# A sixth expert buffer, used once, in the room of the token rows and the last gate

## What is computed

```python
# gates: sigmoid routing, top 8 of 64 experts for each token, plus one shared expert
act = silu(einsum('nd,edf->nef', t, w_gate_e)) * einsum('nd,edf->nef', t, w_up_e) * gates[:, :, None]
routed = einsum('nef,efd->nd', act, w_down_e)
x = x + m[:, 5] * (routed + shared)        # m[:, 5] is "the last gate"
y = rmsnorm(x, final_g)
```

## Time and profile before

| what | us |
|---|---|
| median of three runs | 889.63 |
| lowest and highest of them | 885.89 and 891.04 |
| the profiled execution | 885.69 |
| its span, first to last instruction | 883.9 |
| PE busy | 836.7 (95%) |
| DVE busy | 478.7 (54%) |
| ACT busy | 234.9 (27%) |

### The profile page before, as it was taken

One profiled execution on the slowest core, in us unless ns is written; L12 is line 12 of the kernel. 1 busy time (PEld: TensorE's weight loads), 2 busy tenths in 40 slices (PEclk: granted clock), 3 DMA queues, 4 the chain that ended last, 5 costly groups with the idle time before them and its releaser, 6 DMA issues.

```text
span 883.9 us, 13285 instructions
## 1 busy us (share of the span) xinstructions
PE 836.7 (95%) x4926; PEld 492.6 (56%) x4926; DVE 478.7 (54%) x994; ACT 234.9 (27%) x384; POOL 87.7 (10%) x201
## 2 busy tenths in 40 slices
PE   4799999999999999999999999999999999999993
PEld 2387886889999874444444444444444443444441
DVE  1563373586667456145746454554645454555575
ACT  2537643444423241211111111111111111112122
POOL 7420000000001161000000000000000000000000
PEclk9899999999999999999999999999999999999997
DMA  9984877822244378489999999999999999999951
GB/s 360 353 281 159 315 262 281 195 95 96 96 143 165 158 292 322 178 358 420 421 417 422 418 420 419 419 419 421 419 419 420 419 421 417 421 419 419 420 238 71
DMA packets 70988, 283.06 MB, mean 320 GB/s; under 512 B 14340, under 2 KB 30784, under 8 KB 43920
## 3 DMA queue, kind: packets, MB, share of 16 engines
q1 hardware_dynamic: 55344, 260.06, 73.6%
q0 software_dynamic: 6880, 17.64, 5.4%
q10 hardware_dynamic: 8704, 4.54, 2.0%
HBM read 281.40 MB, written 5.53 MB: 325 GB/s over the span
## 4 chain that ended last, share of the span: by engine, by line
PE 77%; DMA 16%; DVE 3%; issue 1%; POOL 1%; ACT 1%; SPq 0%; POOLq 0%; DVEq 0%; ACTq 0%
PE bank L1444 22%; DMA gu<-in_w_up_e_dram 11%; PE bank L1463 10%; PE bank L1472 8%; PE bank L1074 8%; PE bank L1076 7%; PE bank L1075 7%; DMA chunk_raw<-in_w_ada_dram 3%; PE bank L1432 3%; PE bank L1096 2%; PE bank L1129 1%; DMA h_dram<-h_row 1%; PE bank L1360 1%; PE bank L1552 1%; DMA xg<-h_dram,slot_tok 1%
## 5 line engine op out<-in xcount | busy, mean ns | idle before, releaser
L1444 PE MATMUL bank<-gu,x_t 128*32 128x512 f32 (+2 forms) x1440 | 233.6, 594 | 7.1 <-DMA gu<-in_w_up_e_dram 6.7
L1444 PEld LDWEIGHTS bank<-gu,x_t 128*32 128x32 f32 (+2 forms) x1440 | 74.5, 122 | 149.0 <-issue 143.4
L2068 DVE TENSOR_TENSOR ffn_acc<-ffn_acc,bank 128x512 f32<-128x512 f32 x186 | 116.5, 682 | 7.8 <-PE bank L1472 6.8
L1463 PE MATMUL bank<-dn,a_t 128*32 128x512 f32 (+2 forms) x720 | 120.3, 596 | 0.0
L1036 ACT ACTIVATE silu_sb<-bank 128x256 f32<-128x256 f32 x33 | 12.7, 385 | 320.3 <-PE bank L1444 320.3
L2010 DVE TENSOR_TENSOR act_sb<-silu_sb,bank 128x256 f32<-128x256 f32 x33 | 13.9, 421 | 148.2 <-ACT silu_sb L1036 148.2
L1074 PE MATMUL bank<-h_hi,chunk_lo 128*128 128x384 f32 x240 | 84.0, 350 | 0.0
L1076 PE MATMUL bank<-h_hi,chunk_hi 128*128 128x384 f32 x240 | 80.6, 336 | 0.0
L1075 PE MATMUL bank<-h_lo,chunk_hi 128*128 128x384 f32 x240 | 80.4, 335 | 0.0
L447 DVE TENSOR_TENSOR chunk_lo<-chunk_raw,chunk_hi 128x2048 fp32r<-128x2048 f32 x25 | 57.1, 2289 | 41.5 <-ACT chunk_hi L441 41.3
L2060 DVE SCALAR_TENSOR_TENSOR y_lo<-bank,slot_gate,y_hi 128x512 fp32r<-128x512 f32 x66 | 49.4, 748 | 54.4 <-ACT y_hi L1026 54.2
(11 more groups left out here) (349 smaller groups left out, 1018.2 us busy)
## 6 DMA issues: line engine op xcount, KB each, us to landing
gu<-in_w_gate_e_dram SPq DMA_DIRECT2D x64, 1024.0 KB, 18.6
gu<-in_w_up_e_dram SPq DMA_DIRECT2D x64, 1024.0 KB, 22.3
dn<-in_w_down_e_dram SPq DMA_DIRECT2D x64, 1024.0 KB, 21.6
chunk_raw<-in_w_ada_dram SPq DMA_DIRECT2D x24, 1024.0 KB, 9.0
chunk_raw<-in_w_in_dram SPq DMA_DIRECT2D x18, 1024.0 KB, 6.6
chunk_raw<-in_w_out_dram SPq DMA_DIRECT2D x4, 1024.0 KB, 5.2
chunk_raw<-in_w_pa_dram SPq DMA_DIRECT2D x2, 1024.0 KB, 5.1
chunk_raw<-in_w_pb_dram SPq DMA_DIRECT2D x2, 1024.0 KB, 5.2
```

What stands on the lines that cost most here:

```text
L1444: mm = pe.matmul(bank[2 + odd(u, first)][at_x, :].rearrange("p (g n) -> p g n", g=2), x_t[:, cols], wide[:, :, k, :], start=(k == 0), stop ...
L1463: mm = pe.matmul(outs[half][at_x, :], a_t[:, cols], dn[slot_of(x, first)][:, wc], start=(k == 0), stop=(k == 1))
L2068: dve.tensor_tensor(ffn_acc[t][:, cols], ffn_acc[t][:, cols], out[:, :], ALU.add).then_inc(S["place_out"], 1)
```

## The change

A sixth buffer, `gu_once` and `dn_once` (number RING = 5), is laid over `x_sb`, `gate_ffn` and `final_g_sb`: each of gate and up takes 8 KB and each half of down 4 KB, in two pieces 24 KB apart. It is used for expert x = 3 alone, the fourth that SP loads. All later experts of the first group take the ring's buffers one place earlier in turn, so that expert 5 gets the shared expert's buffer and expert 6 the one of expert 0. From expert 9 on each expert waits for the same predecessor as before.

For that the tokens' rows are stored to a new DRAM tensor `x_dram` (three DMAs on SP's queue behind the first nine loads), and `load_gu` of expert 3 waits for these stores and for `xhat2`. In the last group, behind all gate and up loads and all but the last two down loads, SP loads the last gate, the three token tiles and `final_g` into their places (3 MiB in all; gate and final_g in buffer 2, once expert 10 of that group is done with it). `sums_in` waits for all five. POOL's and ACT's early loads of the two are gone.

```diff
+        gu_once = at("gu_once", [P, 2, 6 * D], 0)
+        dn_once = at("dn_once", [P, 2, 6 * D], 8)
...
+        gate_ffn = at("gate_ffn", [P, 2, D], ring[2])
+        final_g_sb = at("final_g_sb", [P, D], ring[2] + 8)
...
-        SLOT0 = [(0, 3, 1, 4, 2)[x % RING] for x in range(EPG0)]
-        SLOT = [(0, 3, 1, 4, 2)[(EPG0 + x) % RING] for x in range(EPG)]
+        IN_TURN, ONCE = (0, 3, 1, 2, 4), 3
+        SLOT0 = [RING if x == ONCE else IN_TURN[(x - (x > ONCE)) % RING] for x in range(EPG0)]
+        SLOT = [IN_TURN[(EPG0 - 1 + x) % RING] for x in range(EPG)]
...
+                    elif k == RING:
+                        sp.wait_ge(S["xhat2"], TT)
+                        sp.wait_ge(S["out_stored"], 16 * TT)
...
+            for t in range(TT):
+                sp.wait_ge(S["out_done"], TT + t + 1)
+                sp.dma_start(x_dram[t * P:(t + 1) * P, :], x_sb[:, t, :]).then_inc(S["out_stored"], 16)
             sp.wait_ge(S["passes_ready"], 1)
...
+            free = max(x for x in range(EPG) if SLOT[x] == 2)
+            sp.wait_ge(S["gu_used"], last_group(passes) * EPG + (EXPERTS_AHEAD + free + 1))
+            sp.sem_inc(S["turn_step"], 1)
+            sp.dma_start(gate_ffn[:, :, :], gate_dram[:, D:2 * D].unsqueeze(0).to_broadcast([P, 2, D])).then_inc(S["ffn_gate_loaded"], 16)
+            for t in range(TT):
+                sp.dma_start(x_sb[:, t, :], x_dram[t * P:(t + 1) * P, :]).then_inc(S["ffn_gate_loaded"], 16)
+            sp.dma_start(final_g_sb[:, :], final_g.rearrange("(a n) -> a n", a=1).to_broadcast([P, D])).then_inc(S["ffn_gate_loaded"], 16)
             for x, n in sides_of(BPG - 1, False):
                 load_dn(x, last_group(passes), expert_at(bass.ds(last_group(passes) * (2 * BPG) + (SEQ_AHEAD + n), 1)))
...
-            pool.wait_ge(S["w_mm"], NPROJ)
-            spread_rows(gate_ffn, 1, S["ffn_gate_loaded"])
...
-            act.dma_start(final_g_sb[:, :], final_g.rearrange("(a n) -> a n", a=1).to_broadcast([P, D])).then_inc(S["late_loaded"], 16)
...
-                dve.wait_ge(S["ffn_gate_loaded"], 16)
+                dve.wait_ge(S["ffn_gate_loaded"], 16 * (TT + 2))
```

More of the change, by code:

```diff
@@ L265, in hybrid_step @@
         ffn = [at(f"ffn{t}", [P, D], EX + 4 * t) for t in range(TT)]
-        squared = [at(f"squared{t}", [P, D], EX + 24 + 4 * t) for t in range(TT)]
+        gate_ffn = at("gate_ffn", [P, 2, D], ring[2])
+        final_g_sb = at("final_g_sb", [P, D], ring[2] + 8)
+        squared = [at(f"squared{t}", [P, D], EX + 36 + 4 * t) for t in range(TT)]
         place_r = at("place_r", [P, NTOK], EX + 112, F32R)
@@ L329, in hybrid_step @@
         rows_loaded = [sem(f"rows_loaded{t}") for t in range(TT)]
-        gu_ready = [sem(f"gu_ready{i}") for i in range(RING)]
-        dn_ready = [sem(f"dn_ready{i}") for i in range(RING)]
+        gu_ready = [sem(f"gu_ready{i}") for i in range(RING + 1)]
+        dn_ready = [sem(f"dn_ready{i}") for i in range(RING + 1)]
         block = ctx.enter_context(nc.Block())
@@ L526, in load_dn @@
                     sp.wait_ge(S["dn_used"], group * EPG + (EXPERTS_AHEAD + y + 1))
-                    sp.sem_inc(S["sp_turn"], 1)
-                sp.dma_start(dn[k][:, :], w_down_e[0, e].rearrange("a (p k) n -> (a p) (k n)", k=2)).then_inc(dn_ready[k], 16)
+                    sp.sem_inc(S["turn_step"], 1)
+                src = w_down_e[0, e]
+                if k == RING:
+                    sp.dma_start(dn_once[:, :, 0:D], src.rearrange("a (p k) n -> (a p) k n", k=2)).then_inc(dn_ready[k], 16)
+                else:
+                    sp.dma_start(dn[k][:, :], src.rearrange("a (p k) n -> (a p) (k n)", k=2)).then_inc(dn_ready[k], 16)
             def expert_at(n):
@@ L1440, in gate_up @@
                     for x in experts:
-                        wide = gu[slot_of(x, first)][:, :].rearrange("p (g k n) -> p g k n", g=2, n=FE)
+                        wide = gate_up_part(slot_of(x, first))
                         for at_x in tiles_of(x, u, first):
@@ L1459, in down @@
                         for x in experts:
-                            wc = slice(k * D + 512 * half, k * D + 512 * half + 512)
                             for at_x in tiles_of(x, u, first):
                                 cols = slice(k * CAP + at_x.start, k * CAP + at_x.stop)
-                                mm = pe.matmul(outs[half][at_x, :], a_t[:, cols], dn[slot_of(x, first)][:, wc], start=(k == 0), stop=(k == 1))
+                                mm = pe.matmul(outs[half][at_x, :], a_t[:, cols], down_part(slot_of(x, first))[:, k, 512 * half:512 * half + 512], start=(k == 0), stop=(k == 1))
                             if half == 1 and k == 1:
```

27 lines of the change are left out of this document (15 added, 12 removed).

## The result

| | before | after |
|---|---|---|
| median of the runs beside each other, us | 887.88 (883.77 to 892.39, 14 runs) | 895.91 (891.02 to 899.73, 14 runs) |
| ratio | | 1.0092 (95%: 1.0074 to 1.0111) |
| profiled execution, us; its span | 885.69; 883.9 | 896.92; 895.1 |
| granted clock, mean | 0.988 | 0.977 |

The kernel is slower by 0.92%, 8.2 us, where the sum said 5.9. The predicted 895.5 is met more closely than it deserves: the base came out 1.75 us lower (887.88 instead of 889.63) and the difference some 2 us larger. The two profiled executions lie 11.2 us apart, more than the medians: that of before is 2.2 us under its median, that of after 1.0 over.

What follows compares the result with a forecast made beforehand. It took the kernel as bound by DMA and PE streams of nearly equal length, with DVE's sums on the chain at the end. End wait +3.4, clock +1.5 and start +1.0 gave +5.9 on 889.63: 895.5 us, range 888.5 to 901.5.

Steps and rivals of the forecast that it cites:

- the sum: Whole kernel: end wait +3.4, clock +1.5 and start +1.0 make +5.9 us; this forecast had chance 0.60.
- The wait at the end: DVE's first sum waits for the five loads: 7.35 us of loads less a lead of 4.0, +3.4 us (+2.7 to +4.4).
- The lead: DMA stream's gain from the sixth buffer: 7.35 us at 379 us, 4.0 left (3.0 to 4.7) after a new hole.
- load for load: From the new hole at about 403 us on, the stream is full and unchanged, so the lead of 4.0 us holds.
- The clock: Behind PE's gap of about 7 us before the last `act_sb` matmuls, half clock costs +1.5 us (0 to 3.0).
- The row taken for it: PE idle 2.68 us before its first gather transposes, then at half clock: 0.9 + 0.7, about +1.5 us.
- The start: Token-row stores meet the `h_row` stores and delay the first gather and PE: +1.0 us (0 to 3.7).
- Loads hidden: Rival, chance 0.08: the end's five loads land beside the weights and the middle's waits go; faster, 882.9 us.
- No new hole: Rival, chance 0.17: no DMA hole at 399 to 403 us, so the lead of 7.35 pays the five loads; 890.6 us.
- Full price: Rival, chance 0.15: token rows go ahead of `h_row`, +3.7, clock +3.0, end wait +4.4; +11.1 us, 900.7 us.

Runs made afterwards that it cites:

- filled_at_end: The kernel after without the five loads: POOL fills the three tiles with ones and DVE waits for these fills; ratio to before 1.0000, 0.0 us.
- experiment 5: The run fill_hole: the kernel after with the down loads of experts 6 and 7 ahead of expert 9's gate and up load; +9.5 us over before.
- experiment 2: The run loads_only: the kernel before plus the stores and the five loads, no sixth buffer; +12.8 us over before.
- keep_clock: The kernel after with eleven matmuls without use on PE while it waits for the last `act_sb`; ratio to before 1.0060, +5.3 us.
- loads_only: The kernel before plus the token-row stores and the five loads, moved tiles in their old places, no sixth buffer; ratio to before 1.0144, +12.8 us.
- fill_hole: The kernel after with the down loads of experts 6 and 7 ahead of expert 9's gate and up load; ratio to before 1.0107, +9.5 us.
- late_store: The kernel after with the three token-row stores behind the gate and up loads that follow the first nine; ratio to before 1.0077, +6.8 us.
- store_only: The kernel before plus only the three token-row stores, nothing read back; ratio to before 1.0022, +2.0 us.
- pool_queue: The kernel after with the five loads issued from POOL's queue when buffer 2 comes free; ratio to before 1.0086, +7.6 us.
- experiment 8: The run before_reorder: the kernel before with the third token tile's sums behind the last block's steps; +0.4 us over before.
- split_waits: The kernel after with one wait per token tile instead of one for all five, `final_g_sb` loaded and waited for behind the sums; ratio to before 1.0048, +4.3 us.
- before_reorder: The kernel before with the third token tile's two sums behind the last block's steps; ratio to before 1.0005, +0.4 us.
- best: The kernel after with split_waits, late_store and fill_hole combined, `final_g_sb` loaded last, only tile 0's sums ahead of the last steps; ratios to before 0.9985 and 0.9946.

## Why the prediction was right or wrong

**The wait at the end: right in mechanism, and in the price of the loads.** The five loads stand behind the weights (the last lands 19.9 us after its issue), take 7.5 us for the 7.35 said, and DVE, `act_sb` and PE start later by the same 8.9 us. filled_at_end shows that all the loss hangs on them.

**The lead: right at its origin, smaller at the end in the traces.** It was 4.7 us at expert 9, one end of what was said (3.0 to 4.7). It did not hold "load for load": "after that the stream is full and the same" is the sentence that failed. One load of each kernel from 431 us on and one near the end, tile `gu`, the second load of a pair, first before:

```profile
L515 SPq DMA_DIRECT2D gu<-in_w_up_e_dram x1: 382/382/382, 431.7 to 431.7; - x1
...
DMA to landing us min/median/max: 14.3/14.3/14.3
...
L515 SPq DMA_DIRECT2D gu<-in_w_up_e_dram x1: 377/377/377, 827.0 to 827.0; - x1
...
DMA to landing us min/median/max: 19.6/19.6/19.6
```

and after:

```profile
L534 SPq DMA_DIRECT2D gu<-in_w_up_e_dram x1: 387/387/387, 435.0 to 435.0; - x1
...
DMA to landing us min/median/max: 10.4/10.4/10.4
...
L534 SPq DMA_DIRECT2D gu<-in_w_up_e_dram x1: 383/383/383, 827.1 to 827.1; - x1
...
DMA to landing us min/median/max: 20.6/20.6/20.6
```

The first land at 446.0 and 445.4. Against a stage that began 3.3 us later the lead is 3.9 us and no longer 4.8: after the hole at 402 to 406 came a second, smaller one (share 0.81 over 422 to 424; experiment 5 shows such a second hole more strongly). At 827 the landing is 1.1 us later than before (847.7 against 846.6), so the lead is 2.2, and at the down load of 831.2 it is 852.7 against 851.5, 2.1. Where the 1.7 us in between went is open: both streams move 419 GB/s from 446 to 840. The medians speak for a lead of 4.6 (experiment 2), as said. I can't settle which is nearer.

**The clock: right in mechanism, and about right in size.** +1.5 said (ends 0 and 3.0), 2.3 in the trace, 2.2 shown by keep_clock. From DVE's first sum to the end of the span it is 32.5 us before, 34.8 and 35.1 in the two traces of after, but 33.6 in loads_only, 33.7 in fill_hole and 34.1 in late_store, with gaps on PE of 7.7 to 9.2 us in all five: 1.1 to 2.6 us. The row taken for it was of a gap of 2.7 us; this gap was of 9.0, longer than the 7 said, because the first sum came later.

**The start: right in kind, perhaps too small.** +1.0 said, +2.0 by the runs of store_only (0.1 to 3.8). In the trace of after it is 3.3 us: 0.7 before the stores can matter, the stretch from the issue of the last `h_row` store to PE 1.4 longer, and 1.1 of a longer slow stretch. This last was not in the sum at all: the half clock was counted only for the end. It isn't clearly a price of the change either, since with the same stores at the start the stretch is the short one in fill_hole and pool_queue (below).

**The sum.** In the runs 8.2 (6.6 to 9.9) instead of 5.9; the clock (+0.8 by the trace) and the start (+1.0) would account for 1.8 of the 2.3, but neither is measured that finely. In the traces 11.2 instead of 5.9: the start +2.3, the lead 1.9 less, the five loads +0.15 and the clock +0.8 are 5.2 of 5.3. How much of the start's 2.3 is the change's can't be read from one trace: experiment 8 moved it by 4.2 us with nothing changed there.

**The rivals.** Loads hidden: fell with the first trace and with pool_queue, where early loads made the up matrix late. No new hole: fell with the window at 402 to 406. Full price: not reached in the runs, though the start's 3.3 us in the trace is near its 3.7, and the two traces differ by 11.2 us, just its +11.1. Whoever had only the two traces would have called that rival right, and the 14 runs of each say 8.2.

## What to carry to other kernels

Where the DMA stream and an engine are equally long, a buffer that must be handed back costs its bytes at the end, and what it gives at the beginning is partly lost at the next place where the ring makes the loads wait: price both in matrices before building it. Wait for such data tile by tile and put the use of each behind what others wait for; here that, with changes of order on SP, did away with 8 us of loss and likely gave a small gain (1.3 and 4.8 us in two measurements). Count a gap of several us on PE twice: the gap, and the slow stretch that it brings.

## What the runs showed that I had not expected

- **The slow stretch does not follow the length of the gap.** The mean clock of the windows tells how long it was at half: before, with 2.7 us of idle time, 0.79 over the 8 us from 353, which is 8 x 0.21 / 0.5 = 3.4 us; after, with 4.1 us, 0.67 over the same 8 us and 0.63 over 361 to 363, 5.3 + 1.5 = 6.8 us. That looks like a rule, but the other traces don't bear it out: at the same place fill_hole waited 3.93 us and was slow for 3.4, split_waits waited 3.40 us and was slow for 6.8. One row gives the size of such a cost only to within a factor of two.
- **Landings of loads that share a semaphore are not to be read one by one.** By the trace of after the gate's load (issued at 832.0, 18.2 us to landing, so 850.2) overtook the down load issued before it (831.2, landed 852.7). But all five loads count up one semaphore there, and the profile gives each the next 16 of its steps, whichever load they came from. In split_waits the gate has a semaphore of its own, and lands 2.5 us behind the down load (856.5 against 854.0), the first token tile 1.3 us later: in order, as the prediction had it. Of a group on one semaphore only the last landing is sure.

```profile
L550 SPq DMA_DIRECT2D dn<-in_w_down_e_dram x1: 333/333/333, 833.6 to 833.6; - x1
...
DMA to landing us min/median/max: 20.4/20.4/20.4
...
L589 SPq DMA_DIRECT2D gate_ffn<-gate_dram x1: 388/388/388, 834.4 to 834.4; - x1
...
DMA to landing us min/median/max: 22.1/22.1/22.1
```

- **The start of a stage wanders.** Kernels with the same instructions up to there began the experts' transposes between 354.94 and 359.12 (before and before_reorder), and best, twice the same program, at 354.08 and 358.84. A difference of 4 us between two single traces is no evidence until the same point of both has been subtracted.
- **A hole moved on.** Filling the one at 402 opened another 15 us later, one block on (fill_hole).
